# Finer first chunks, a small first parameter load, and two vector steps moved into the retention

## The chip, the cores and the metric

The kernel runs on one core of a Trainium2 chip. The metric is the device time of one execution in microseconds (us). TensorE is PE in the profile, VectorE DVE, ScalarE ACT, GpSimd POOL and SyncE SP.

## The reference

Two blocks of a language model are computed one after the other for 256 tokens of width 1024, in float32. The first puts 16 meta tokens ahead of the input, normalises the rows, and projects them to queries, keys, values and gates; it has a retention with rotary positions (8 heads of 128), a recurrence, and a feed-forward part. The second has three more mixing branches and a mixture of experts. What the change touches stands at the beginning of the first block:

```
h = concatenate([meta, x])                      # 272 rows
u = h * rsqrt(mean(h * h) + eps) * mix_norm_w   # first norm
q, k, v, g_ret, lru_in, ... = split(u @ w_in)
q, k = rotary(q), rotary(k)
o = chunk_retention(q, k, v)                    # per head: scores, decay, scores @ v
c = causal_depthwise_conv(lru_in)               # 4 taps
r = rg_lru(c, ..., lru_lambda)                  # uses softplus(-lru_lambda)
```

## The kernel before

Every matrix product is made of three matmuls: each operand is split into a high and a low half (`whi`, `wlo` for weights), and high x high, high x low and low x high are summed in a PSUM bank. The weights come as pieces of 1 MB, 128 x 2048 floats, in the fixed order of the table `PIECES` ("k" 4 pieces, "q" 4, "v" 4, "lru_in" 4, "g_ret" 4, ...), into three slots of `raw`. SP issues the transfer of a piece once the slot's old piece is split. ACT rounds it to `whi` (line 1136 in `round_piece`), DVE subtracts to get `wlo` (L1667 in `split_piece`), and PE waits for that split. ACT and DVE do this inside their own programs, which are written out by hand: `feed(engine, n)` splits all pieces up to n at that point of the engine's order, and `full(engine, n)` also waits until PE has used n pieces.

**The start.** PE first runs 19 dummy matmuls (L630). Piece 0 and the transposed input `x_t` are loaded in four chunks (L520, L521), each of two of the eight 128-row feature blocks. For a chunk ACT scales the two blocks of x by the first norm's weights (`W("mixw")`) and rounds them, then rounds a quarter of piece 0; DVE makes both low halves (L1714, L1717); `early_keys` on PE multiplies the chunk. All parameters (`par`, 161 columns, "mixw" the first 8) are loaded by one transfer on ACT's queue (L1177), for which ACT and DVE wait. Piece 1 is split in two halves (L1719, L1721). SP queues, in this order, the chunks, pieces 1 and 2, the identity, the two halves of x, the meta tokens, the other constants and the narrow weights `small_w`. ACT squares x row by row for the norm, DVE makes the inverse roots (L1708), and PE spreads them over a row in `scale_row` (L666, L668), behind the products of piece 1. DVE scales the rotary tables by that row.

**The v products.** After the rotations of q DVE calls `rest_of_head` (L1737): it scales the router columns of the narrow weights (L1740), waits for ACT's rounding of them, subtracts (L1742), and computes the recurrence constant softplus(-lambda) as a chain of small instructions on 128 x 8 elements, each waiting for the last (L1745 to L1757). Only then does `feed(dve, PB["lru_in"] + p + 1)` split further pieces. ACT's part, `narrow_high`, lies at the corresponding place of its own order.

**The retention.** A loop over four pairs of heads, p = 0 to 3. PE makes the scores of two heads, the input product of the recurrence for piece `lru_in` + p (li banks), and then scores times v (L712 to L715, bank `o.p`), for which it waits until the score banks are scaled. DVE for each p: `feed` (the split of a piece), the scaling of both heads' scores (L1790 to L1792, three instructions for a head), from p = 1 a reduction (L1796), then, once ACT has copied the li banks, the convolution of two blocks (L1800, L1802). ACT rounds the convolved blocks and after that the next weight piece, which DVE's `feed` of the next p waits for. The constant is read by ACT much later, behind the recurrence's gates (wait for `lam_ready`); the narrow low half `swlo` by GpSimd's first squares of the retention (as a wait) and by PE in the second block.

Of the kernel before, what the change touches and what calls it, by code (L numbers as in the profile page):

```python
# [5 lines left out]
P = 128  # L6
# [3 lines left out]
KT = D // P  # L10
META = 16
TM = META + T
# [14 lines left out]

PIECES = [("k", 4), ("q", 4), ("v", 4), ("lru_in", 4), ("g_ret", 4), ("lru_gates", 2), ("lru_gate", 4),
# [128 lines left out]
PC, NPAR = columns(PARAMS)  # L157
# [45 lines left out]
def program(nc, weights, x, x_t, meta, mem, consts, params, small_w, slot_w, final_w, wa2_w, out):  # L203
# [8 lines left out]
    with ExitStack() as ctx:  # L212
# [72 lines left out]
        def bc1(a, n):  # L285
# [8 lines left out]
        chunk_loaded = [sem(f"chunk_loaded{j}") for j in range(4)]  # L294
# [10 lines left out]
        meta_loaded, ident_loaded, par_loaded, wa2_loaded, small_loaded = (  # L305
            sem(n) for n in ("meta_loaded", "ident_loaded", "par_loaded", "wa2_loaded", "small_loaded"))
# [254 lines left out]
        def _(pe):  # L561
# [89 lines left out]
            def early_keys(n, names, parts, waits):  # L651
                w = [part.rearrange("p (k c) -> p k c", k=KT) for part in (whi[:, n, :], wlo[:, n, :])]
                outs = [begin(x) for x in names]
                size = KT // parts
                for j in range(parts):
                    pe.wait_ge(*waits(j))
                    for c in range(2):
                        for k in range(size * j, size * (j + 1)):
                            last = product(outs[c][:, 0:TM], both(w, ALL, k, slice(c * P, (c + 1) * P)), both(XU, ALL, k), k == 0, k == KT - 1)
                last.then_inc(pieces_used, 1)  # L660
# [16 lines left out]
            early_keys(0, ["k.0", "k.1"], 4, lambda j: (early_split, j + 1) if j < 3 else (piece_split, 1))  # L677
            early_keys(1, ["k.2", "k.3"], 2, lambda j: (early_split, 4) if j == 0 else (piece_split, 2))
# [453 lines left out]
        def _(act):  # L1132
# [44 lines left out]
            act.dma_start(par[:, :], params).then_inc(par_loaded, 16)  # L1177
            act.wait_ge(zeros_ready, 1)
            A(warmed, zeros[:, 0:1], ACT.Sqrt)
            act.wait_ge(par_loaded, 16)  # L1180
            for j in range(4):
                act.wait_ge(chunk_loaded[j], 32 if j < 3 else 16)
                for k in (2 * j, 2 * j + 1):
                    last = A(XU[0][:, k, :], XR[:, k, :], ACT.Copy, scale=W("mixw")[:, k:k + 1])
                last.then_inc(x_high, 1)
                if j == 3:
                    act.wait_ge(piece_loaded[0], 16)
                quarter = slice(512 * j, 512 * (j + 1))
                A(whi[:, 0, quarter], raw[:, 0, quarter], ACT.Copy).then_inc(early_high if j < 3 else piece_high, 1)
# [466 lines left out]
        def _(dve):  # L1656
# [53 lines left out]
            dve.wait_ge(par_loaded, 16)  # L1710
            for j in range(4):
                dve.wait_ge(x_high, j + 1)
                for k in (2 * j, 2 * j + 1):
                    V.scalar_tensor_tensor(XU[1][:, k, :], XR[:, k, :], W("mixw")[:, k:k + 1], XU[0][:, k, :].bitcast(f32), mult, sub)  # L1714
                dve.wait_ge(*((early_high, j + 1) if j < 3 else (piece_high, 1)))
                quarter = slice(512 * j, 512 * (j + 1))
                V.tensor_tensor(wlo[:, 0, quarter], raw[:, 0, quarter], whi[:, 0, quarter].bitcast(f32), sub).then_inc(early_split if j < 3 else piece_split, 1)  # L1717
            dve.wait_ge(early_high, 4)
# [51 lines left out]
            for k in range(KT):  # L1770
                last = V.scalar_tensor_tensor(XR[:, k, :], XR[:, k, :], W("mixw")[:, k:k + 1], SROW, mult, mult)
            last.then_inc(x_scaled, 1)
            for p in range(4):
                full(dve, PB["q"] + p + 1)
                if p == 1:
                    dve.wait_ge(x_high, 5)
                    V.tensor_tensor(XT[1][:, :, :], XR, XT[0][:, :, :].bitcast(f32), sub).then_inc(x_scaled, 1)
# [3 lines left out]
            rest_of_head()  # L1781

            for p in range(4):
# [9 lines left out]

                if p:
# [724 lines left out]
```

## Time and profile before

| | us |
|---|---|
| median of 3 runs (lowest, highest) | 1081.66 (1081.64, 1082.83) |
| the profiled execution | 1081.13 |
| its span | 1079.0 |
| PE busy | 1066.6 |
| DVE busy | 730.3 |
| ACT busy | 620.0 |

The span goes from the first to the last instruction that the profiler saw; the execution's own time has some 2 us around it. Matmuls are pipelined, so that a busy PE is not PE at its peak, but where PE stands idle the time is lost for the whole kernel if all behind it moves by as much.

### The profile page before, as it was taken

The page shows a single profiled execution, that of the slowest core. Times are in us where ns is not written, and L with a number is a line of the kernel's source. Part 1 is how long each engine was busy: PE and PEld are TensorE (multiplying, and loading weights), DVE is VectorE, ACT ScalarE, POOL GpSimd, SP SyncE. Part 2 cuts the span into 40 slices and gives each one's busy share as a digit, 9 for nine tenths or more (in the row PEclk, how much of TensorE's full clock was granted, in tenths as well). Part 3 has the DMA queues.
Part 4 walks back from the last instruction along what each step waited for, and adds up shares of the span by engine and source line. Part 5 has one row for each costly group of instructions (what it writes and reads, how often), then busy time and mean ns, then how long its engine had stood idle before and what let it go on. Part 6 is the DMA issues. An engine that isn't in the chain of part 4 may idle for free.

```text
span 1079.0 us, 17108 instructions
## 1 busy us (share of the span) xinstructions
PE 1066.6 (99%) x7014; PEld 954.9 (88%) x7014; DVE 730.3 (68%) x823; ACT 620.0 (57%) x735; POOL 52.4 (5%) x41
## 2 busy tenths in 40 slices
PE   9999999999999999999999999999999999999998
PEld 7998889999989999998898777889999978878886
DVE  5974665865765554545765648895445678899996
ACT  7753369664465444443673437775444467777774
POOL 0420100000000000000000000000000002000000
PEclk9999999999999999999999999999999999999999
DMA  9552254654745555555346433434446457999993
GB/s 352 201 196 78 79 195 157 232 199 156 247 164 196 197 193 194 194 194 195 117 157 217 158 99 112 151 124 154 160 169 219 167 198 270 355 381 387 366 396 109
DMA packets 32929, 218.04 MB, mean 202 GB/s; under 512 B 4416, under 2 KB 4672, under 8 KB 7520
## 3 DMA queue, kind: packets, MB, share of 16 engines
q1 hardware_dynamic: 30688, 212.96, 55.1%
q0 software_dynamic: 1616, 2.66, 0.7%
q10 hardware_dynamic: 560, 1.47, 0.3%
q8 instruction: 50, 0.82, 0.3%
q14 instruction: 15, 0.12, 0.0%
HBM read 216.55 MB, written 3.67 MB: 204 GB/s over the span
## 4 chain that ended last, share of the span: by engine, by line
PE 91%; DVE 6%; ACT 1%; DMA 1%; issue 1%; SPq 0%; POOLq 0%; DVEq 0%; ACTq 0%
PE bank L578 27%; PE bank L580 27%; PE bank L579 27%; PE bank L639 2%; DVE wlo L1664 1%; DVE wlo L1667 1%; DMA raw<-weights_dram 1%; PE bank L1045 1%; PE bank L967 1%; PE bank L949 1%; DVE last_lo L1664 1%; PE bank L715 0%; PE bank L880 0%; PE bank L1097 0%; PE bank L712 0%
## 5 line engine op out<-in xcount | busy, mean ns | idle before, releaser
L1667 DVE TENSOR_TENSOR wlo<-raw,whi 128x2048 fp32r<-128x2048 f32 x137 | 313.5, 2294 | 161.1 <-ACT whi L1136 160.8
L1136 ACT ACTIVATE whi<-raw 128x2048 fp32r<-128x2048 f32 (+1 forms) x171 | 319.8, 1875 | 136.3 <-PE bank L580 129.2
L578 PE MATMUL bank<-normedT_hi,whi 128*128 128x256 f32 x640 | 177.6, 278 | 0.0
L579 PE MATMUL bank<-normedT_lo,whi 128*128 128x256 f32 x640 | 177.0, 277 | 0.0
L580 PE MATMUL bank<-normedT_hi,wlo 128*128 128x256 f32 x640 | 177.0, 277 | 0.0
L1136 ACT ACTIVATE buf<-bank 128x512 f32<-128x512 f32 (+5 forms) x147 | 70.9, 526 | 145.9 <-PE bank L580 120.2
L578 PEld LDWEIGHTS bank<-normedT_hi,whi 128*128 128x128 f32 x640 | 120.1, 188 | 1.0 <-issue 0.6
L579 PEld LDWEIGHTS bank<-normedT_lo,whi 128*128 128x128 f32 x640 | 120.3, 188 | 0.7 <-issue 0.2
L580 PEld LDWEIGHTS bank<-normedT_hi,wlo 128*128 128x128 f32 x640 | 120.3, 188 | 0.0
L578 PE MATMUL bank<-xT_hi,whi 128*128 128x256 f32 (+1 forms) x320 | 90.9, 284 | 1.7 <-DVE wlo L1667 1.7
L579 PE MATMUL bank<-xT_lo,whi 128*128 128x256 f32 (+1 forms) x320 | 90.2, 282 | 0.0
L580 PE MATMUL bank<-xT_hi,wlo 128*128 128x256 f32 (+1 forms) x320 | 90.2, 282 | 0.0
L1664 DVE TENSOR_TENSOR wlo<-raw,whi 128x2048 fp32r<-128x2048 f32 x27 | 61.7, 2288 | 5.0 <-ACT whi L1136 5.0
L578 PEld LDWEIGHTS bank<-xT_hi,whi 128*128 128x128 f32 x320 | 60.1, 188 | 3.2 <-DVE wlo L1667 1.9
L579 PEld LDWEIGHTS bank<-xT_lo,whi 128*128 128x128 f32 x320 | 60.2, 188 | 0.0
L580 PEld LDWEIGHTS bank<-xT_hi,wlo 128*128 128x128 f32 x320 | 60.2, 188 | 0.0
L578 PE MATMUL bank<-whi,normedT_hi 128*128 128x512 f32 x144 | 57.6, 400 | 0.4 <-DVE wlo L1667 0.3
L580 PE MATMUL bank<-whi,normedT_lo 128*128 128x512 f32 x144 | 56.5, 392 | 0.0
L579 PE MATMUL bank<-wlo,normedT_hi 128*128 128x512 f32 x144 | 56.4, 392 | 0.0
L578 PE MATMUL bank<-whi,gathered_hi 128*128 128x512 f32 x128 | 51.3, 401 | 0.0
L580 PE MATMUL bank<-whi,gathered_lo 128*128 128x512 f32 x128 | 50.0, 391 | 0.0
L579 PE MATMUL bank<-wlo,gathered_hi 128*128 128x512 f32 x128 | 49.9, 390 | 0.0
(415 smaller groups left out, 2412.9 us busy)
## 6 DMA issues: line engine op xcount, KB each, us to landing
raw<-weights_dram SPq DMA_DIRECT2D x174, 1024.0 KB, 5.0
buf<-weights_dram SPq DMA_DIRECT2D x24, 1024.0 KB, 7.3
buf<-x_t_dram SPq DMA_DIRECT2D x4, 272.0 KB, 4.8
raw<-weights_dram SPq DMA_DIRECT2D x4, 256.0 KB, 5.9
buf<-x_dram SPq DMA_DIRECT2D x2, 512.0 KB, 11.2
buf<-mem_dram ACTq DMA_DIRECT2D x1, 1024.0 KB, 10.7
token_rows<-buf SPq DMA_DIRECT2D x1, 1024.0 KB, 8.7
buf<-final_w_dram POOLq DMA_DIRECT2D x1, 512.0 KB, 4.2
```

What stands on the lines that cost most here:

```text
L578: E.matmul(out_, lh, rh, start=start, stop=False)
L579: E.matmul(out_, lh, rl, start=False, stop=False)
L580: return E.matmul(out_, ll, rh, start=False, stop=stop)
L639: last = E.transpose(b[0:i.shape[1], o:o + n], i, ident[0:n, 0:n])
L949: last = E.matmul(b[:, hh * T:(hh + 1) * T], MQT[:, 2 * h + k, r * P:(r + 1) * P], MKT[:, 2 * h + k, :], start=k == 0, stop=k == 1)
L967: last = E.matmul(b[:, c * T:(c + 1) * T], MV[:, s, h * T + c * P:h * T + (c + 1) * P], MPT[:, h, s, :], start=s == 0, stop=s == 1)
L1045: last = E.matmul(o, part[:, r, k * P:(k + 1) * P], PICK[:, r, lo:hi], start=r == 0 and i == 0, stop=r == RT - 1 and i == 1)
L1136: return S.activation(out_, in_, func, **kw)
L1664: V.tensor_tensor(WLO[split_of(u)], RAW[raw_of(u)], WHI[split_of(u)].bitcast(f32), sub).then_inc(piece_split, 1)
L1667: V.tensor_tensor(wlo[:, n % SLOTS, :], raw[:, n % SLOTS, :], whi[:, n % SLOTS, :].bitcast(f32), sub).then_inc(piece_split, 1)
```

## The change

- The table `EARLY` gives the chunks of the start: one, one, two, two and two feature blocks in place of two each. Loads, ACT's and DVE's splits and PE's `early_keys` go over it. The split of piece 1 in halves stays.
- The transfer on ACT's queue brings only the first norm's weights, 8 columns, to a place of their own (`MIXW`). The full parameters are loaded by SP, behind the identity and ahead of x. DVE waits for them in `narrow_scaled`.
- `rest_of_head` is cut in three. The scaling stays behind the rotations of q; the narrow low half (`narrow_low`) goes into the first pair of the retention (p = 0), and the recurrence constant (`recurrence_constant`) into the third (p = 2), both behind the scaling of the scores.

```diff
--- before.py
+++ after.py
@@ -25,6 +25,7 @@
+EARLY = [range(0, 1), range(1, 2), range(2, 4), range(4, 6), range(6, 8)]
...
+        HEAD = buf[5][:, 0:KT * TM]
         XR = cols(5, TM)
+        MIXW = place("mixw", fixed_at[-1] + starts[4] + 1024 + TM, KT)
...
         @block.sync
         def _(sp):
-            for j in range(4):
-                pair_, quarter = slice(2 * j, 2 * j + 2), slice(512 * j, 512 * (j + 1))
-                sp.dma_start(XR[:, pair_, :], x_t[:, pair_, :]).then_inc(chunk_loaded[j], 16)
-                sp.dma_start(raw[:, 0, quarter], weights[0][:, quarter]).then_inc(chunk_loaded[j] if j < 3 else piece_loaded[0], 16)
+            for j, ks in enumerate(EARLY):
+                cols_, part = slice(ks[0] * TM, (ks[-1] + 1) * TM), slice(256 * ks[0], 256 * (ks[-1] + 1))
+                sp.dma_start(HEAD[:, cols_], x_t[:, cols_]).then_inc(chunk_loaded[j], 16)
+                sp.dma_start(raw[:, 0, part], weights[0][:, part]).then_inc(chunk_loaded[j] if j < len(EARLY) - 1 else piece_loaded[0], 16)
             for n in (1, 2):
                 sp.dma_start(raw[:, n, :], weights[n]).then_inc(piece_loaded[n], 16)
             sp.dma_start(con[:, 0:P], consts[:, 0:P]).then_inc(ident_loaded, 16)
+            sp.dma_start(par[:, :], params).then_inc(par_loaded, 16)
             for r in range(RT):
...
-            early_keys(0, ["k.0", "k.1"], 4, lambda j: (early_split, j + 1) if j < 3 else (piece_split, 1))
-            early_keys(1, ["k.2", "k.3"], 2, lambda j: (early_split, 4) if j == 0 else (piece_split, 2))
+            early_keys(0, ["k.0", "k.1"], EARLY, lambda j: (early_split, j + 1) if j < len(EARLY) - 1 else (piece_split, 1))
+            early_keys(1, ["k.2", "k.3"], [range(0, 4), range(4, 8)], lambda j: (early_split, len(EARLY)) if j == 0 else (piece_split, 2))
...
-            act.dma_start(par[:, :], params).then_inc(par_loaded, 16)
+            act.dma_start(MIXW[:, :], params[:, PC["mixw"][0]:PC["mixw"][1]]).then_inc(mixw_loaded, 16)
             act.wait_ge(zeros_ready, 1)
             A(warmed, zeros[:, 0:1], ACT.Sqrt)
-            act.wait_ge(par_loaded, 16)
-            for j in range(4):
-                act.wait_ge(chunk_loaded[j], 32 if j < 3 else 16)
-                for k in (2 * j, 2 * j + 1):
-                    last = A(XU[0][:, k, :], XR[:, k, :], ACT.Copy, scale=W("mixw")[:, k:k + 1])
+            act.wait_ge(mixw_loaded, 16)
+            for j, ks in enumerate(EARLY):
+                act.wait_ge(chunk_loaded[j], 32 if j < len(EARLY) - 1 else 16)
+                for k in ks:
+                    last = A(XU[0][:, k, :], XR[:, k, :], ACT.Copy, scale=MIXW[:, k:k + 1])
                 last.then_inc(x_high, 1)
...
-            def rest_of_head():
+            def narrow_scaled():
+                dve.wait_ge(par_loaded, 16)
                 dve.wait_ge(small_loaded, 16)
                 router = SWR.rearrange("p (k c) -> p k c", k=KT)[:, :, 88:108]
                 V.tensor_tensor(router, router, bc(W("gffn"), 20), mult).then_inc(small_scaled, 1)
+
+            def narrow_low():
                 dve.wait_ge(small_high, 1)
                 V.tensor_tensor(swlo[:, :], SWR, swhi[:, :].bitcast(f32), sub).then_inc(small_split, 1)
+
+            def recurrence_constant():
                 dve.wait_ge(lam_exp, 1)
...
-            rest_of_head()
+            narrow_scaled()
 
             for p in range(4):
                 feed(dve, PB["lru_in"] + p + 1)
...
+                if p == 0:
+                    narrow_low()
+                if p == 2:
+                    recurrence_constant()
                 if p:
                     dve.wait_ge(o_squared, p)
```

DVE's order behind the rotations of q, before (`par` are the parameters, `small` the small statistics, `buf_71` the narrow weights):

```order
L1764 TENSOR_TENSOR buf_70<-buf_62,con 128x512
L1740 TENSOR_TENSOR buf_71<-buf_71,par 128x8x20 [waits small_loaded]
L1742 TENSOR_TENSOR swlo<-buf_71,swhi 128x864 [waits small_high]
L1745 TENSOR_SCALAR small<-small 128x8 [waits lam_exp]
L1746 RECIPROCAL small<-small 128x8 [waits dve_chain]
...
L1756 TENSOR_SCALAR small<-small 128x8 [waits dve_chain]
L1757 TENSOR_SCALAR small<-small 128x8
L1667 TENSOR_TENSOR wlo<-raw,whi 128x2048 [waits piece_high] x4
L1790 TENSOR_SCALAR buf_69<-bank,con 128x128 [waits scored]
```

and now:

```order
L1772 TENSOR_TENSOR buf_70<-buf_62,con 128x512
L1744 TENSOR_TENSOR buf_71<-buf_71,par 128x8x20 [waits small_loaded,par_loaded]
L1670 TENSOR_TENSOR wlo<-raw,whi 128x2048 [waits piece_high] x4
L1798 TENSOR_SCALAR buf_69<-bank,con 128x128 [waits scored]
L1799 SCALAR_TENSOR_TENSOR buf_69<-bank,con 128x128
L1800 SCALAR_TENSOR_TENSOR buf_69<-bank,con 128x128
```

The low half and the whole chain on 128 x 8 elements are gone from between the scaling of the router columns and the splits.

DVE's order in the third pair of heads, from the end of the first score scaling of its second head, before (`buf_69` scaled scores, `buf_66` and `buf_70` input and result of the convolution):

```order
L1790 TENSOR_SCALAR buf_69<-bank,con 128x128 [waits retained,scored]
L1791 SCALAR_TENSOR_TENSOR buf_69<-bank,con 128x128
L1792 SCALAR_TENSOR_TENSOR buf_69<-bank,con 128x128
L1796 TENSOR_REDUCE small<-buf_71 128x2x2 [waits o_squared]
L1800 TENSOR_SCALAR buf_70<-buf_66,par 128x272 [waits evacuated7,evacuated6]
L1802 SCALAR_TENSOR_TENSOR buf_70<-buf_66,par,buf_70 128x272 [waits dve_chain] x3
...
L1667 TENSOR_TENSOR wlo<-raw,whi 128x2048 [waits piece_high]
L1790 TENSOR_SCALAR buf_69<-bank,con 128x128 [waits retained,scored]
```

and now:

```order
L1798 TENSOR_SCALAR buf_69<-bank,con 128x128 [waits retained,scored]
L1799 SCALAR_TENSOR_TENSOR buf_69<-bank,con 128x128
L1800 SCALAR_TENSOR_TENSOR buf_69<-bank,con 128x128
L1753 TENSOR_SCALAR small<-small 128x8 [waits lam_exp]
L1754 RECIPROCAL small<-small 128x8 [waits dve_chain]
...
L1764 TENSOR_SCALAR small<-small 128x8 [waits dve_chain]
L1765 TENSOR_SCALAR small<-small 128x8
L1808 TENSOR_REDUCE small<-buf_71 128x2x2 [waits o_squared]
L1812 TENSOR_SCALAR buf_70<-buf_66,par 128x272 [waits evacuated7,evacuated6]
...
L1670 TENSOR_TENSOR wlo<-raw,whi 128x2048 [waits piece_high]
```

The chain stands between the scaled scores and the reduction, ahead of this pair's convolution and of the split that follows it.

## Rows read from the trace of the kernel before

**Rows 1.** Page, part 1, and busy time by stretch at 61 to 71 us (PE clock third from last)
```profile
span 1079.0 us, 17108 instructions
...
PE 1066.6 (99%) x7014; PEld 954.9 (88%) x7014; DVE 730.3 (68%) x823; ACT 620.0 (57%) x735; POOL 52.4 (5%) x41
...
61.00:71.00 10.00, 8.34 (x67) 8.10 (x66) 7.63 (x28) 8.83 (x12) 1.31 (x1) 1.00 0.23 94
```

**Rows 2.** Waits of PE: us in total, times, longest us
```profile
PE bank L578 <- DVE wlo L1667: 2.7, 4, 1.7
...
PE bank L578 <- DVE wlo L1719: 0.3, 1, 0.3
```

**Rows 3.** Timeline, 0 to 22 us: start, duration, engine, line, operation, [idle before]
```profile
0.96 7.20 PE L630 MATMUL bank<-idle 128*128 128x512 bf16 x19 [0.96 <-POOL idle L2387]
...
13.07 2.01 ACT L1136 ACTIVATE whi<-raw 128x1024 fp32r<-128x1024 f32 x2 [1.04 <-DMA raw<-weights_dram]
...
14.17 1.23 DVE L1719 TENSOR_TENSOR wlo<-raw,whi 128x1024 fp32r<-128x1024 f32 x1 [1.03 <-ACT whi L1136]
...
15.45 0.40 PE L578 MATMUL bank<-xU_hi,whi 128*128 128x272 f32 x1 [0.32 <-DVE wlo L1719]
...
18.81 1.06 ACT L1136 ACTIVATE buf<-buf 128x1024 f32<-128x1024 f32 x1 [0.23 <-DMA buf<-x_dram]
...
21.12 0.47 DVE L1708 RECIPROCAL small<-small 128x1 f32<-128x1 f32 x3
...
21.74 0.37 PE L666 MATMUL bank<-con,small 16*128 16x16 f32 x2
```

**Rows 4.** DMA queues in 3-3.5, 5.5-6 and 8-9 us: packets, MB, share of 16 engines
```profile
q10 hardware_dynamic: 69, 0.03, 23.9%
...
q1 hardware_dynamic: 60, 0.11, 93.3%
...
q1 hardware_dynamic: 200, 0.41, 108.9%
```

**Rows 5.** Timeline of DVE, 60 to 76 us
```profile
60.88 0.31 DVE L1740 TENSOR_TENSOR buf<-buf,par 128x160 f32<-128x160 f32 x1
...
62.25 1.06 DVE L1742 TENSOR_TENSOR swlo<-buf,swhi 128x864 fp32r<-128x864 f32 x1 [1.06 <-ACT swhi L1136]
...
63.87 0.17 DVE L1745 TENSOR_SCALAR small<-small 128x8 f32<-128x8 f32 x1 [0.56 <-ACT small L1136]
...
68.51 0.17 DVE L1757 TENSOR_SCALAR small<-small 128x8 f32<-128x8 f32 x1
...
68.58 6.69 DVE L1667 TENSOR_TENSOR wlo<-raw,whi 128x2048 fp32r<-128x2048 f32 x3
```

**Rows 6.** Timeline of ACT and of PE, 63 to 71 us
```profile
63.74 1.90 ACT L1136 ACTIVATE whi<-raw 128x2048 fp32r<-128x2048 f32 x1
...
68.67 0.60 PE L639 MATMUL bank<-con,buf 128*128 128x128 f32 x4
...
70.92 0.39 PE L578 MATMUL bank<-xT_hi,whi 128*128 128x272 f32 x1 [1.66 <-DVE wlo L1667]
```

**Rows 7.** Timeline of DVE, 94 to 133 us (retention)
```profile
94.86 0.42 DVE L1800 TENSOR_SCALAR buf<-buf,par 128x272 f32<-128x272 f32 x1 [7.88 <-ACT buf L1136]
...
117.45 0.67 DVE L1796 TENSOR_REDUCE small<-buf 128x4 f32<-128x512 f32 x1
...
119.50 0.42 DVE L1800 TENSOR_SCALAR buf<-buf,par 128x272 f32<-128x272 f32 x1 [1.38 <-ACT buf L1136]
...
129.52 0.34 DVE L1792 SCALAR_TENSOR_TENSOR buf<-bank,con 128x128 f32<-128x128 f32 x1
...
131.82 0.42 DVE L1800 TENSOR_SCALAR buf<-buf,par 128x272 f32<-128x272 f32 x1 [1.37 <-ACT buf L1136]
```

**Rows 8.** Timeline of PE, 130 to 141 us
```profile
130.71 0.29 PE L580 MATMUL bank<-xT_hi,wlo 128*128 128x272 f32 x1
...
140.68 0.50 PE L578 MATMUL bank<-whi,xT_hi 128*128 128x512 f32 x1 [0.41 <-DVE wlo L1667]
```

More of the change, by code:

```diff
@@ L293, in program @@
         piece_high = sem("piece_high")
-        chunk_loaded = [sem(f"chunk_loaded{j}") for j in range(4)]
+        chunk_loaded = [sem(f"chunk_loaded{j}") for j in range(len(EARLY))]
         early_high, early_split = sem("early_high"), sem("early_split")
@@ L304, in program @@
         x_loaded = [sem(f"x_loaded{r}") for r in range(RT)]
-        meta_loaded, ident_loaded, par_loaded, wa2_loaded, small_loaded = (
-            sem(n) for n in ("meta_loaded", "ident_loaded", "par_loaded", "wa2_loaded", "small_loaded"))
+        meta_loaded, ident_loaded, par_loaded, wa2_loaded, small_loaded, mixw_loaded = (
+            sem(n) for n in ("meta_loaded", "ident_loaded", "par_loaded", "wa2_loaded", "small_loaded", "mixw_loaded"))
         out_stored = sem("out_stored")
@@ L653, in early_keys @@
                 outs = [begin(x) for x in names]
-                size = KT // parts
-                for j in range(parts):
+                for j, ks in enumerate(parts):
                     pe.wait_ge(*waits(j))
                     for c in range(2):
-                        for k in range(size * j, size * (j + 1)):
+                        for k in ks:
                             last = product(outs[c][:, 0:TM], both(w, ALL, k, slice(c * P, (c + 1) * P)), both(XU, ALL, k), k == 0, k == KT - 1)
@@ L1175, in turned_high @@
                     last.then_inc(high[name], 1)
-            act.dma_start(par[:, :], params).then_inc(par_loaded, 16)
+            act.dma_start(MIXW[:, :], params[:, PC["mixw"][0]:PC["mixw"][1]]).then_inc(mixw_loaded, 16)
             act.wait_ge(zeros_ready, 1)
             A(warmed, zeros[:, 0:1], ACT.Sqrt)
-            act.wait_ge(par_loaded, 16)
-            for j in range(4):
-                act.wait_ge(chunk_loaded[j], 32 if j < 3 else 16)
-                for k in (2 * j, 2 * j + 1):
-                    last = A(XU[0][:, k, :], XR[:, k, :], ACT.Copy, scale=W("mixw")[:, k:k + 1])
+            act.wait_ge(mixw_loaded, 16)
+            for j, ks in enumerate(EARLY):
+                act.wait_ge(chunk_loaded[j], 32 if j < len(EARLY) - 1 else 16)
+                for k in ks:
+                    last = A(XU[0][:, k, :], XR[:, k, :], ACT.Copy, scale=MIXW[:, k:k + 1])
                 last.then_inc(x_high, 1)
-                if j == 3:
+                if j == len(EARLY) - 1:
                     act.wait_ge(piece_loaded[0], 16)
-                quarter = slice(512 * j, 512 * (j + 1))
-                A(whi[:, 0, quarter], raw[:, 0, quarter], ACT.Copy).then_inc(early_high if j < 3 else piece_high, 1)
+                part = slice(256 * ks[0], 256 * (ks[-1] + 1))
+                A(whi[:, 0, part], raw[:, 0, part], ACT.Copy).then_inc(early_high if j < len(EARLY) - 1 else piece_high, 1)
             act.wait_ge(piece_loaded[1], 16)
@@ L1708, in x_inverse @@
                 V.reciprocal(s, s).then_inc(x_scaled, 1)
-            dve.wait_ge(par_loaded, 16)
-            for j in range(4):
+            dve.wait_ge(mixw_loaded, 16)
+            for j, ks in enumerate(EARLY):
                 dve.wait_ge(x_high, j + 1)
[L1713 to L1718, printed above, removed]
+                for k in ks:
+                    V.scalar_tensor_tensor(XU[1][:, k, :], XR[:, k, :], MIXW[:, k:k + 1], XU[0][:, k, :].bitcast(f32), mult, sub)
+                dve.wait_ge(*((early_high, j + 1) if j < len(EARLY) - 1 else (piece_high, 1)))
+                part = slice(256 * ks[0], 256 * (ks[-1] + 1))
+                V.tensor_tensor(wlo[:, 0, part], raw[:, 0, part], whi[:, 0, part].bitcast(f32), sub).then_inc(early_split if j < len(EARLY) - 1 else piece_split, 1)
+            dve.wait_ge(early_high, len(EARLY))
             V.tensor_tensor(wlo[:, 1, 0:PW // 2], raw[:, 1, 0:PW // 2], whi[:, 1, 0:PW // 2].bitcast(f32), sub).then_inc(early_split, 1)
@@ L1770, in _ @@
             for k in range(KT):
-                last = V.scalar_tensor_tensor(XR[:, k, :], XR[:, k, :], W("mixw")[:, k:k + 1], SROW, mult, mult)
+                last = V.scalar_tensor_tensor(XR[:, k, :], XR[:, k, :], MIXW[:, k:k + 1], SROW, mult, mult)
             last.then_inc(x_scaled, 1)
@@ L1775, in _ @@
                 if p == 1:
-                    dve.wait_ge(x_high, 5)
+                    dve.wait_ge(x_high, len(EARLY) + 1)
                     V.tensor_tensor(XT[1][:, :, :], XR, XT[0][:, :, :].bitcast(f32), sub).then_inc(x_scaled, 1)
```

2 lines of the change are left out of this document (1 added, 1 removed).

## The prediction

> **What bounds the kernel now.** I read the page first: the span is 1079.0 us and TensorE (PE) is busy for 1066.6 of them [rows 1]. So this change can give back only time in which PE stands still in the first 140 us, or add such time. The waits of PE are the next view: over the whole span the longest single one is 1.7 us, on a `wlo` split of VectorE (DVE); on the half piece of the start it is 0.3 [rows 2]. Three places matter.
>
> The start: PE runs 19 dummy matmuls from 0.96 for 7.20 us, to 8.16. Later ScalarE (ACT) rounds the first half of piece 1 at 13.07, after 1.04 us idle until its transfer landed; DVE subtracts at 14.17, and PE begins that piece at 15.45. ACT squares the second half of x at 18.81, after 0.23 us idle for its transfer; the third reciprocal of DVE ends at 21.12 + 0.47 = 21.59, and PE takes the scales at 21.74 [rows 3]. So from 13 us on the start goes at the pace of the transfers. The second place is the v products: DVE works on the narrow weights and the recurrence constant from 60.88 to 68.58, only then splits, and PE, whose transposes began at 68.67, takes its next piece at 70.92 after 1.66 us idle [rows 5, 6]. The third is the retention, at 94 to 141 us, where PE hardly waits [rows 7, 8].
>
> **Chunks of one, one, two, two, two.** The first chunk has half the bytes, so PE could have work by about 7 us. But the 19 dummy matmuls stand ahead of it until 8.16 and their number is unchanged; the products of piece 0 then run out early, and PE waits longer for piece 1. What counts is when piece 1 lands. The change puts 4 transfers with rows of about 1 KB in the place of 2 with rows of 2 KB: 512 packets for 256, 16 more for each of the 16 DMA engines. Their price comes from two rows: 69 packets of the parameter load (644 B each) took 23.9% of 16 engines for 0.5 us, 28 ns each; 200 packets of about 2 KB took 108.9% of 16 engines for 1 us, 87 ns each [rows 4]. The line through both has a fixed part of 0 to 5 ns; counting gaps between small issues I take 0.2 us for 16 packets (bounds 0, and 16 x 87 = 1.4 us if a half packet costs as much as a whole). Against that, the parameter load leaves the front: 8 packets each engine x 28 ns = 0.2 us, of which 8 packets of 32 B take back about as much again, since no row shows packets that small (0 to 0.2). Piece 1 comes at +0.2.
>
> SyncE now issues the full parameter load ahead of x, which puts its 0.2 us in front of both x transfers: x comes at +0.4 to +0.5. ACT already waits 0.23 us for x, and the reciprocals end 0.15 us before PE starts on the scales [rows 3], so nearly all of this reaches PE: **+0.45 us** (bounds -0.3, if the small first packets save time at the head of the queue, and +1.7). The extra ACT and DVE instructions of the finer chunks (one more rounding and one more subtraction) are covered by ACT's 1.04 us idle before 13.07; without that cover they would cost some 0.2 us on ACT.
>
> The Trainium skill speaks against small transfers: "DMA: Bandwidth & Descriptors", in Bandwidth, gives a 64 KB transfer 0.95 us and one of 1 MB 6.15 us; an estimate between them gives 1.3 us for 128 KB and 2.0 for 256 KB, so four small in place of two large would cost 1.3 us where I take 0.2, and the sum below would be 1.1 us higher. Its figures are for another issuing engine, and no run here shows them.
>
> **The narrow low half and the constant leave the place after q.** `narrow_scaled` stays at 60.88 and ACT's part behind it too, so ACT still rounds the piece from 63.74 to 65.64 [rows 6]. DVE stood in its own constant until 68.58 [rows 5]; now it can start the split at about 65.7 and ends it 2.29 us later (one split's time, the first part of the 6.69 for three), at 67.95. PE needs it after its four transposes, at 68.67 + 0.6 = 69.27. The whole wait of **-1.66 us** goes, with 1.3 us to spare. Nothing is late next: the following split ends at about 70.3, one full product before its use.
>
> **The narrow low half, in the first retention pair.** It lands behind the six score scalings, in front of the convolution, where DVE idles 7.88 us until 94.86 [rows 7]; 1.06 us of work [rows 5] costs nothing. Without that cover it would delay the convolution by 1.06 us. GpSimd's squares wait for it, but also for a later ACT result.
>
> **The recurrence constant, in the third pair.** From its first instruction at 63.87 to the split behind it at 68.58 it holds DVE for 4.71 us: 24 instructions of some 0.17 us, nearly all waiting for the one before [rows 5]. It goes in front of the reduction that began at 117.45. Between that reduction and the convolution at 119.50 DVE had only 1.38 us idle [rows 7]. So the reduction begins at 117.45 + 4.71 = 122.16, and the convolution 0.67 later, at 122.83: 3.33 us late. Everything behind it hangs in one chain: ACT's rounding of the convolved pair, ACT's rounding of a weight piece, DVE's split of it, and then the six score scalings of the fourth pair, whose last was at 129.52 + 0.34 = 129.86. It moves to 133.19. PE's product with these scores followed its last input product at 130.71 + 0.13 (one matmul every 0.13 us) = 130.84 [rows 8]. A new wait of 133.19 - 130.84 = 2.35 us stands there.
>
> Part is given back: DVE's reduction of 0.67 comes between, so the fourth convolution goes from 131.82 to 133.86, 2.0 late and not 2.35, and the piece that PE waited 0.41 us for at 140.68 [rows 8] comes 2.0 late too. PE arrives 2.35 later than before, less than 0.1 from it. The 0.41 is thus covered, and the net is 2.35 - 0.4 = **+1.97 us**. Its bounds: 0, if PE turns out not to need these scores first, and 3.33, if the delay of DVE passes whole.
>
> **Sum**, on the profiled execution (1081.13 us): +0.45 - 1.66 + 1.97 = +0.76, so 1081.9. The median of the three runs is 0.5 us above the profiled one, and the measure is taken there: 1081.66 + 0.76 = **1082.4 us**. A measurement of this kernel can tell about 0.2%, or 2.2 us, from no change; this isn't that much.
>
> **Rivals.**
> - *The constant is hidden.* If PE does not come to the fourth pair's scores before DVE has made them, the third term is 0 and the sum is +0.45 - 1.66 = -1.2: 1080.5 us. For it: PE showed no wait at all in the retention before 140 us. Against it: the order puts the constant ahead of the reduction, and the slack is 130.84 - 129.86 = 1.0 us behind a delay of 3.33. Chance 0.13.
> - *Slower: the start is bound by the number of packets.* If a 1 KB packet takes what a 2 KB one does, the 16 more cost 16 x 104 = 1.7 us, at a time between 87 ns and the (93.3% of 16 engines for 0.5 us) / 60 = 124 ns of 5.5 to 6 us [rows 4]; with 0.2 for the parameters +1.9, and the sum is +1.9 - 1.66 + 1.97 = +2.2: 1083.9 us. It decides where x lands over 1.5 us later. For it: in 5.5 to 6 us packets of the same size took 124 ns against 87, so bytes alone don't set their time. Against it: the 28 ns of the 644 B packets. The figures of the Trainium skill given above point the same way. Chance 0.11.
> - *The start gains as well.* If the transfers of the start land 0.6 us earlier and the constant is hidden, -1.66 - 0.6 = -2.3: 1079.4 us. It needs x itself to come earlier, though more stands before it. Chance 0.04.
> - *The clock falls in the new wait.* The granted clock was 1.00 in the stretch that held the 1.66 us wait [rows 1], the upper of the two levels; 2.35 us is longer than any wait shown. One product of 48 matmuls at the lower level would cost its own 48 x 0.13 = 6.2 us again: some 1088 us. Chance 0.03.
>
> **How the numbers follow.** The forecast has 0.69, and its own range is 1081.2 to 1083.6, from +0.1 to +1.1 for the start and a few tenths on the new wait. For 8 in 10 the range takes in half of the first rival and half of the second: 1080.5 to 1084.0; outside are about 0.06, 0.06, 0.04 and 0.03. Faster by over 0.2% (under 1079.5) needs the third rival and part of the first: 0.06. Slower by over 0.2% (over 1083.8) comes from half of the second, the clock and the edge of the forecast: 0.10. The rest, 0.84, is within 0.2%.
>
> **What would show it.** In the profile after: dummy matmuls to 8.16 and the first product right behind; PE's wait before piece 1 longer than before, that piece begun at 15.5 to 15.9; the scales at about 22.2; no wait at the third v product; a new wait of PE of about 2.3 us before the fourth pair's score products (an L712 matmul before, waiting for DVE's score scaling), and none left behind it on the next `wlo`. I am wrong if PE does not wait there (first rival), if x lands more than 1.5 us later (second), or if the wait at the v products is still there.

## The result, and the profile after

| | before | after |
|---|---|---|
| median (lowest to highest), 5 runs each | 1082.53 (1081.64 to 1084.70) | 1088.15 (1088.08 to 1088.47) |
| span of the profiled execution | 1079.0 | 1086.4 |
| PE busy | 1066.6 | 1070.8 |
| mean granted clock of PE | 1.00 | 0.994 |

The ratio is 1.0054 [1.0042, 1.0065]: slower by 5.6 us of medians, and by 7.4 us between the two profiled executions. 1082.4 was forecast, with a range to 1084.0. The waits of PE in the kernel after answer to [rows 2] (us in total, times, longest):

```profile
PE bank L715 <- DVE buf L1800: 3.2, 1, 3.2
PE bank L582 <- DVE wlo L1720: 2.8, 1, 2.8
...
PE bank L582 <- DVE wlo L1670: 0.6, 2, 0.3
```

The wait at the v products is gone (four waits on full pieces, the longest 1.7, are now two of 0.3). Two others stand there, of 3.15 us in the retention and 2.85 in the start, and PE's busy time rose by 4.2 us for the same 7014 matmuls. Busy time by stretch says why (stretch, us, busy time and instructions of PE, PEld, DVE, ACT, POOL, then the granted clock, DMA share and GB/s). The kernel after:

```profile
11.00:14.50 3.50, 3.35 (x15) 3.35 (x16) 3.04 (x7) 2.45 (x6) 0.00 (x0) 0.52 1.00 424
61.00:71.00 10.00, 10.00 (x82) 10.00 (x81) 5.44 (x5) 7.14 (x10) 2.42 (x2) 1.00 0.41 130
134.00:143.00 9.00, 9.00 (x26) 6.72 (x27) 3.99 (x9) 2.36 (x4) 1.44 (x2) 0.50 0.25 103
```

and the kernel before, in the first and the last of these stretches:

```profile
11.00:14.50 3.50, 3.50 (x30) 3.50 (x29) 2.47 (x6) 2.46 (x5) 0.00 (x0) 1.00 0.99 410
...
134.00:143.00 9.00, 8.59 (x38) 6.67 (x37) 6.33 (x8) 7.93 (x8) 2.50 (x2) 1.00 0.15 33
```

In both stretches the clock was 1.00, the upper level (2.4 GHz), and is now 0.50 to 0.52, the lower one (1.2 GHz). PE is busy for all of the 9 us from 134, and does 26 matmuls in them where it did 38. At 61 to 71 us PE stands still no more (10.00 against 8.34 of [rows 1]).

**The start**, timeline of PE, ACT and DVE in the kernel after (answers to [rows 3]):

```profile
0.96 5.83 PE L634 MATMUL bank<-idle 128*128 128x512 bf16 x19 [0.96 <-POOL idle L2399]
...
3.93 0.52 ACT L1139 ACTIVATE xU_hi<-buf,mixw 128x272 fp32r<-128x272 f32 x1 [1.22 <-DMA raw<-weights_dram]
...
6.44 0.48 PE L582 MATMUL bank<-xU_hi,whi 128*128 128x272 f32 x1
...
8.62 0.93 ACT L1139 ACTIVATE xU_hi<-buf,mixw 128x272 fp32r<-128x272 f32 x2 [2.56 <-DMA raw<-weights_dram]
...
11.15 0.60 PE L582 MATMUL bank<-xU_hi,whi 128*128 128x272 f32 x1 [2.85 <-DVE wlo L1720]
...
14.04 2.01 ACT L1139 ACTIVATE whi<-raw 128x1024 fp32r<-128x1024 f32 x2 [1.05 <-DMA raw<-weights_dram]
...
20.09 1.06 ACT L1139 ACTIVATE buf<-buf 128x1024 f32<-128x1024 f32 x1 [0.54 <-DMA buf<-x_dram]
...
22.40 0.47 DVE L1711 RECIPROCAL small<-small 128x1 f32<-128x1 f32 x3
...
23.41 0.39 PE L669 MATMUL bank<-con,small 16*128 16x16 f32 x2
```

The first chunk is there early (ACT takes it at 3.93), the third only at 8.62. ACT waits for transfers all along, and piece 1 comes 0.97 us later than before (14.04 for 13.07), the second half of x 1.28 (20.09 for 18.81), the scales 1.67 (23.41 for 21.74).

**The retention**, timeline of DVE, POOL and PE in the third and fourth pair, the kernel after (answers to [rows 7, 8]; the last row is from behind the retention):

```profile
117.22 0.17 DVE L1753 TENSOR_SCALAR small<-small 128x8 f32<-128x8 f32 x1
...
121.92 0.68 DVE L1808 TENSOR_REDUCE small<-buf 128x4 f32<-128x512 f32 x1
...
122.97 2.42 DVE L1814 SCALAR_TENSOR_TENSOR buf<-buf,par,buf 128x272 f32<-128x272 f32 x3
122.98 1.04 POOL L2413 TENSOR_TENSOR buf<-buf 128x512 f32<-128x512 f32 x1 [9.83 <-ACT buf L1139]
...
125.77 1.57 DVE L1814 SCALAR_TENSOR_TENSOR buf<-buf,par,buf 128x272 f32<-128x272 f32 x3
...
130.49 0.29 PE L584 MATMUL bank<-xT_hi,wlo 128*128 128x272 f32 x1
...
133.38 0.34 DVE L1800 SCALAR_TENSOR_TENSOR buf<-bank,con 128x128 f32<-128x128 f32 x1
...
133.93 0.77 PE L715 MATMUL bank<-buf,buf 128*128 128x128 f32 x2 [3.15 <-DVE buf L1800]
...
166.06 2.29 DVE L1833 TENSOR_TENSOR buf<-buf,buf 128x2048 f32<-128x2048 f32 x1 [2.51 <-ACT buf L1139]
```

The constant's chain takes 121.92 - 117.22 = 4.70 us. Three of the convolution's instructions then take 2.42 us, while GpSimd squares beside them; the next three of the same form take 1.57. PE, in the end 0.22 us ahead of before (130.49 for 130.71), waits 3.15 us. The last row is a landmark: this product of DVE stood at 158.69 in the kernel before. It is 7.37 us late, as much as the whole span, so the loss lies ahead of it. PE's first score product is 133.93 - 130.83 = 3.10 late; between it and the landmark another 4.27 are lost, and the old wait of 0.41 [rows 8] is gone besides: some **4.7 us** are left for the clock. This is a rest by subtraction; e5 below tests it.

### The profile page after: what moved, and what is told of

Read it like the earlier page. It is cut to its first block, busy times and chain, and to the rows that moved or that the text cites. A ratio compares the mean times of both kernels' runs of the same rounds, so it can differ in the third digit from the quotient of the medians.

```text
span 1086.4 us, 17114 instructions
## 1 busy us (share of the span) xinstructions
PE 1070.8 (99%) x7014; PEld 959.4 (88%) x7014; DVE 731.3 (67%) x824; ACT 620.2 (57%) x736; POOL 52.2 (5%) x41
## 4 chain that ended last, share of the span: by engine, by line
PE 91%; DVE 6%; ACT 1%; issue 1%; DMA 1%; SPq 0%; POOLq 0%; DVEq 0%; ACTq 0%
PE bank L582 28%; PE bank L583 27%; PE bank L584 27%; PE bank L643 2%; DVE wlo L1667 1%; PE bank L1048 1%; DVE buf L1814 1%; PE bank L970 1%; PE bank L952 1%; DVE last_lo L1667 1%; DMA raw<-weights_dram 1%; PE bank L883 0%; PE bank L718 0%; PE bank L1100 0%; DVE wlo L1670 0%
## 5 line engine op out<-in xcount | busy, mean ns | idle before, releaser
L1139 ACT ACTIVATE whi<-raw 128x2048 fp32r<-128x2048 f32 (+3 forms) x172 | 320.1, 1866 | 137.4 <-PE bank L584 130.6
## 6 DMA issues: line engine op xcount, KB each, us to landing
buf<-mem_dram ACTq DMA_DIRECT2D x1, 1024.0 KB, 10.5
```

What stands on the lines that cost most here:

```text
L1139: return S.activation(out_, in_, func, **kw)
```

## The experiments

"Old start" is the start of the kernel before. The constant (24 instructions) stands behind q as in the kernel before, or in the first or third pair of the retention.

| | start | constant | median (runs) | ratio to before, 95% |
|---|---|---|---|---|
| e1 | new | first pair | 1081.07 (10) | 0.9991 [0.9981, 1.0001] |
| e2 | old | third pair | 1086.99 (4) | 1.0045 [1.0028, 1.0061] |
| e3 | new | behind q | 1084.36 (6) | 1.0021 [1.0009, 1.0034] |
| e4 | old | first pair | 1080.26 (10) | 0.9983 [0.9973, 0.9993] |
| e5 | old | third pair, 14 dummies in the wait | 1083.09 (10) | 1.0008 [0.9997, 1.0020] |
| e6 | chunks only | behind q | 1083.65 (10) | 1.0013 [1.0004, 1.0023] |
| e7 | small parameter load only | behind q | 1082.71 (10) | 1.0002 [0.9991, 1.0013] |
| e8 | old | 11 instructions in the first, 13 in the third | 1080.96 (10) | 0.9985 [0.9976, 0.9995] |
| e9 | old | third pair, GpSimd's squares later | 1085.26 (5) | 1.0033 [1.0019, 1.0047] |
| e10 | old | third pair, 7 dummies in the wait | 1085.22 (10) | 1.0026 [1.0014, 1.0039] |

### e1, e2, e3 and e4: start and place of the constant, apart

My theory was by now that the constant's place costs most, through PE's wait and the clock behind it; the rival was that the start did it, through late transfers and its own stretch at the lower clock. e1 is the changed kernel with

```diff
                 if p == 0:
                     narrow_low()
-                if p == 2:
                     recurrence_constant()
```

> The changed kernel with the recurrence constant in the first pair of the retention (p = 0) instead of the third. Theory 1 (the loss lies in the constant's place: PE waits 3.15 us in the fourth pair and then runs at half the granted clock for some 8 us, which costs about 4 us more): both are gone, the span falls by about 7 us to 1079 to 1080, the median is 0.0 to 1.0 us below that of the kernel before, no stretch behind 100 us has a clock under 0.95. Rival (the loss lies in the start, whose PE wait of 2.85 us also has a half clock behind it): the time stays above 1086.

e2 is the kernel before with only the three calls of the retention from the change:

```diff
-            rest_of_head()
+            narrow_scaled()
...
+                if p == 0:
+                    narrow_low()
+                if p == 2:
+                    recurrence_constant()
```

> The kernel before with only the retention part of the change: narrow low half at p = 0, recurrence constant at p = 2; chunks and parameter load as before. Theory 1: the wait at the v products (1.66 us) is gone, the wait in the fourth pair (3.1 to 3.3 us) and the half clock behind it (8 us long, 4 us lost) are there without the new start: 5 to 5.5 us slower than before, 1087. Rival (the clock falls there only because the start had lowered it before): the clock stays 1.00 and the result is +1.0 to +1.5 us.

e3 is the changed kernel with both steps back behind `narrow_scaled()`:

> The changed kernel with both steps back behind the rotations of q, so only the chunks and the parameter load are new. Theory 1: PE reaches the scales at 23.4 instead of 21.7 us, +1.7 us, all of which stays: 1083.3 to 1084.2, with a stretch at half clock in 11 to 14 us and the 1.66 us wait at the v products back. Rival (the start costs as much as the whole change): 1088. Second rival (the lateness is absorbed by the wait at the v products): +0.0.

It came to 1084.36 us, just above the range of theory 1. Its profile has the scales at 23.26, a wait of 2.65 us in the start with the clock at 0.50 behind it to about 14 us, and the longest v wait at 1.8 us again.

e4 is e2 with `recurrence_constant()` at p = 0 too:

> The kernel before with narrow low half and constant both in the first pair (p = 0), where DVE idles nearly 8 us. Theory 1: 1.66 to 1.9 us faster than before, 1079.8 to 1080.8, no wait of PE over 0.5 us before 160 us apart from the start. Rival (removing the wait at the v products only moves it on): same as before.

e4 is 6.7 us faster than e2 with the old start (1086.99 - 1080.26), and e1 7.1 faster than the changed kernel with the new one (1088.15 - 1081.07); e1 is even 1.5 us below the kernel before (1082.54), where 0.0 to 1.0 was expected. Nothing but the constant's place differs. e2, with the old start, has the wait and the clock of the changed kernel. First its timeline of PE:

```profile
132.64 0.77 PE L713 MATMUL bank<-buf,buf 128*128 128x128 f32 x2 [3.16 <-DVE buf L1798]
```

and its busy time by stretch:

```profile
134.00:143.00 9.00, 9.00 (x26) 6.82 (x26) 3.19 (x7) 3.64 (x5) 2.35 (x2) 0.50 0.13 55
```

In e4 the same two views, the timeline and then the busy time by stretch, are these; DVE has its 2.19 us of idle time left ahead of the first convolution there, even with the whole chain in that pair.

```profile
139.44 0.51 PE L580 MATMUL bank<-whi,xT_hi 128*128 128x512 f32 x1 [0.41 <-DVE wlo L1668]
```

```profile
134.00:143.00 9.00, 8.59 (x37) 6.70 (x37) 6.36 (x8) 8.51 (x8) 2.51 (x2) 1.00 0.28 86
```

The 0.41 us of [rows 8] is back, the clock is 1.00, and the landmark stands at 157.47. So the wait of 3.15 us together with the lower clock is the loss of the change, and both come from the third pair. e4 has the lowest median of all versions; by the ratios it can't be told from e8 (0.9983 and 0.9985).

The new start costs 1081.07 - 1080.26 = 0.8 us between e4 and e1, 1.2 between e2 and the changed kernel, and 1.8 between the kernel before (1082.54 in that comparison) and e3. Only the last is clear of the spread; the intervals of e1 and e4 overlap, as those of e2 and the changed kernel do. In e1 the dummy matmuls took 7.14 us, PE waited only 0.76 and 0.99 us in the start and kept its clock (busy time by stretch):

```profile
11.00:14.50 3.50, 3.40 (x27) 3.19 (x26) 2.63 (x6) 1.85 (x5) 0.00 (x0) 1.00 1.00 422
```

Still its scales came at 23.44, as in the changed kernel (23.41). The lower clock of the start thus hid behind the transfers; what the start costs is their lateness.

### e6 and e7: which half of the new start

e6 is the kernel before with the table of five chunks alone, all parameters still first; e7 keeps the four chunks and takes the small parameter load with the full one behind the identity:

```diff
-EARLY = [range(0, 2), range(2, 4), range(4, 6), range(6, 8)]
+EARLY = [range(0, 1), range(1, 2), range(2, 4), range(4, 6), range(6, 8)]
```

> The kernel before with the chunks of one, one, two, two, two alone; the full parameters still come first on ACT's queue and both steps stay behind the rotations of q. If the smaller rows make the transfers slow: piece 1 is rounded at 14.0 (before 13.07), x comes about 1 us late, the scales at 22.6 to 23.2, +1 to +1.5 us. Rival (the parameters in front of x cost the time): piece 1 within 0.2 us of before, +0.0 to +0.3 us.

```diff
-            act.dma_start(par[:, :], params).then_inc(par_loaded, 16)
+            act.dma_start(MIXW[:, :], params[:, PC["mixw"][0]:PC["mixw"][1]]).then_inc(mixw_loaded, 16)
...
+            sp.dma_start(par[:, :], params).then_inc(par_loaded, 16)
```

> The kernel before with the small first parameter load alone, chunks of two each, the full parameters ahead of x on SP's queue, both steps behind the rotations of q. If the smaller rows of the chunks were what cost time: piece 1 at 12.8 to 13.1, x +0.3 us, the scales at 22.0 to 22.1: +0.3 us. Rival (the parameters' transfer costs over 1 us where it stands now): the scales at 22.7 or later.

In e6 piece 1 is rounded at 14.16, x is squared at 19.91 and the scales come at 23.17; in e7 these are 13.71, 19.81 and 22.74; before, 13.07, 18.81 and 21.74. So the chunks bring 1.1 us at piece 1, and either half about 1 us at x. One execution is no exact measure of these: the profiles of the six other kernels with the old start (e2, e4, e5, e8, e9, e10) have the scales anywhere from 21.58 to 22.41, and piece 1 rounded from 12.90 to 13.46. The four profiles with the finer chunks (after, e1, e3, e6) lie outside on both, at 23.17 to 23.44 and 13.92 to 14.17. For e7 I had expected piece 1 at 12.8 to 13.1 and the scales at 22.0 to 22.1. It is beyond both, and its scales are where its rival had them, at 22.7 or later; the median shows nothing of it. Over all, the chunks cost 0.13%, and the small load nothing that can be measured.

e7's profile shows something else. It has the old wait at the v products and none in the retention, and yet its clock fell there, in a stretch in which PE had no idle time at all (timeline of PE, e7):

```profile
110.42 0.48 PE L718 MATMUL bank<-buf,buf 16*128 16x128 f32 x2
110.83 1.22 PE L697 MATMUL bank<-buf,buf 128*128 128x256 f32 x2
111.84 0.64 PE L698 MATMUL bank<-buf,buf 128*128 128x128 f32 x2
```

The 128x256 products take 1.22 us for two from 110.83 on, where two took 0.70 in the kernel before. Busy time by stretch:

```profile
112.00:113.00 1.00, 1.00 (x5) 0.91 (x4) 0.12 (x1) 0.84 (x2) 1.00 (x2) 0.50 0.00 0
```

PE had been on the retention's small products since 107.16 us. What this says of the prediction stands further down.

### e5 and e10: idle time or late scores

e5 is e2 with dummy matmuls in the wait, so that PE has something to do, and the scores are as late as in e2; e10 has 7 of them.

```diff
                 b = begin(f"o.{p}")
+                if p == 3:
+                    spin(b, 14)
                 moved(pe, f"s.{2 * p}"
```

> The kernel of e2 (old start, constant in the third pair) with 14 dummy matmuls on PE in front of the wait of the fourth pair, into that pair's own bank. Theory 1 (the wait and the clock behind it are two prices, 3.2 us and 4.1 us, the second because PE stands idle): the dummies of 0.21 us fill 3.0 of the 3.16 us, the clock stays 1.00 behind 131 us, PE starts the pair at the same time after its last input product as in e2, and the time is about 4 us under e2: 1082.5 to 1083.5. Rival (the half clock comes from something else, as DVE or the transfers): the clock falls as in e2, about 1087.

> The kernel of e5 with 7 dummy matmuls in place of 14, so that PE stands idle for some 1.6 us of the 3.16 us wait. The start of the fourth pair doesn't move. If the length of the idle time lets the clock fall: it stays 1.00 (1.66 us before did no harm) and the time is that of e5, 1083. Rival (any unfilled rest of that wait brings the half clock): 1087 as in e2.

Timeline of PE, e5, with the 14 dummies and the first of the scores:

```profile
129.76 3.20 PE L632 MATMUL bank<-idle 128*128 128x512 bf16 x14
132.96 0.46 PE L715 MATMUL bank<-buf,buf 128*128 128x128 f32 x2
```

and busy time by stretch, e5:

```profile
134.00:143.00 9.00, 9.00 (x43) 6.94 (x43) 6.10 (x10) 6.17 (x6) 2.37 (x2) 1.00 0.19 76
```

PE begins with the scores 0.32 us later than in e2, does 43 matmuls in 9 us where e2 did 26, and reaches the landmark at 160.40 instead of 165.52. The median falls by 1086.99 - 1083.09 = 3.9 us. That is what the dummies give back, by runs, and it is rather too little for the clock: only three of e5's ten executions had a mean clock of 1.000, the others 0.996 to 0.999. The profiled executions say 5.4: from the scores to the landmark e5 takes 27.44 us, e2 32.88. The wait alone leaves the kernel at the time of before. The timeline of PE in e10:

```profile
129.46 1.69 PE L632 MATMUL bank<-idle 128*128 128x512 bf16 x7
132.66 0.46 PE L715 MATMUL bank<-buf,buf 128*128 128x128 f32 x2 [1.51 <-DVE buf L1800]
```

and its busy time by stretch:

```profile
137.00:140.00 3.00, 3.00 (x9) 2.32 (x8) 0.31 (x2) 3.00 (x4) 2.35 (x2) 0.51 0.02 5
```

Here PE resumes at the full clock, and the clock falls only some 4 us later, for about 3.5 us. I had expected 1.51 us of idle time to leave it alone, since 1.66 us at the v products does (clock 1.00, [rows 1]). It didn't, and the median lies between the two that I had named (1083 and 1087); the ten runs spread from 1082.40 to 1087.35 us, and the interval overlaps that of e2. So the length of the idle time doesn't decide alone.

### e8 and e9: how much fits, and the collision with GpSimd

e8 leaves the chain's last 13 instructions in the third pair and does the first 11 in the first:

```diff
-                for d in (13, 11, 9, 7, 5, 3, 1):
+                for d in (13, 11, 9):
...
+            def constant_end():
...
+                for d in (7, 5, 3, 1):
```

> Old start; the first 11 of the constant's 24 instructions in the first pair, the last 13 in the third. By the chain's 0.205 us an instruction the third pair's reduction begins 2.65 us late and its convolution 1.3 us late. If DVE and GpSimd get in each other's way there as in the changed kernel (three instructions took 2.42 us in place of 1.58 while GpSimd's squares ran), 2.1 us late, and PE waits 1.1 to 1.3 us; if not, 0.3 us. The clock stays 1.00 in both. Time 1080.5 to 1081.5; rival (every wait there brings the half clock): over 1084.

e9 is e2 with GpSimd's squares of the third pair behind its low half of the convolution:

```diff
+                if p != 2:
+                    squares_of(p)
                 pool.wait_ge(high["conv"], p + 1)
...
+                if p == 2:
+                    squares_of(p)
```

> The kernel of e2 (old start, constant in the third pair) with GpSimd's squares of the third pair moved behind its low half of the convolution, out of the time in which DVE convolves. If GpSimd's squares held DVE up: the three convolution instructions that took 2.42 us take 1.58 again, the wait of the fourth pair falls from 3.16 to 2.3 us. Whether the clock falls behind 2.3 us no run has shown: if it does, the time is 0.8 us under e2, 1086.2; if not, 1082 to 1083. Rival (DVE was held up by something else): 2.42 and 3.16 us as in e2.

In e8 the wait shrinks to 0.67 us, where I had 1.1 to 1.3 with a collision and 0.3 without, and the clock of the profiled execution is 1.00 (timeline of PE, e8):

```profile
130.02 0.46 PE L713 MATMUL bank<-buf,buf 128*128 128x128 f32 x2 [0.67 <-issue]
```

The collision moves with the squares: 0.67 us (2.24 for 1.57) land on the second block's instructions in e8, in e9 none on the convolution, but 0.46 on the split (2.75 for 2.29). Timeline of DVE and POOL in e8:

```profile
119.25 1.57 DVE L1819 SCALAR_TENSOR_TENSOR buf<-buf,par,buf 128x272 f32<-128x272 f32 x3
...
121.19 2.24 DVE L1819 SCALAR_TENSOR_TENSOR buf<-buf,par,buf 128x272 f32<-128x272 f32 x3
121.56 1.04 POOL L2418 TENSOR_TENSOR buf<-buf 128x512 f32<-128x512 f32 x1 [9.83 <-ACT buf L1137]
```

and in e9:

```profile
122.04 1.57 DVE L1812 SCALAR_TENSOR_TENSOR buf<-buf,par,buf 128x272 f32<-128x272 f32 x3
...
127.65 1.04 POOL L2412 TENSOR_TENSOR buf<-buf 128x512 f32<-128x512 f32 x1
128.09 2.75 DVE L1668 TENSOR_TENSOR wlo<-raw,whi 128x2048 fp32r<-128x2048 f32 x1 [2.53 <-ACT whi L1137]
```

Three times over, a GpSimd operation of 1.04 us takes 0.84, 0.67 or 0.46 us from what DVE does at that moment. The Trainium skill says this in "SBUF — State Buffer", Who interferes with whom: a DVE instruction with two inputs in SBUF and a GpSimd instruction that reads SBUF exclude each other, and whoever comes first holds the port. These traces agree: all DVE instructions here that grew have two such inputs. In e9 the wait is still 2.75 us and not the 2.3 I had expected, since the squares now hold up the split; PE resumes at the full clock at 132.60, which falls at about 134.5 and is 0.50 until about 141. The time, too, lies between the two that I had named. It is 1.7 us of medians below e2 (1086.99 - 1085.26), but with 4 and 5 runs the intervals overlap.

## Why the prediction was wrong

- **What bounds the kernel: right.** All of the 7.4 us lie in the first 166 us, in PE's idle time and clock.
- **v products, -1.66: right.** The wait is gone, and PE's balance from the scales (+1.67) to the end of the fourth input product (-0.22) says -1.89, a bit more than the term. DVE began the split at 67.38, and PE its transposes at 70.36 (68.67 before): both are 1.7 us later than said, by what the start lost, and the order between them held.
- **Low half in the first pair, 0: right.** It stands at 86.68 in an idle stretch; DVE idled 6.91 us where it had 7.88.
- **Start, +0.45: mis-sized, it is +1.67** in the profile and 0.8 to 1.8 us in medians. The step that failed is "Piece 1 comes at +0.2": it came 0.97 us late after the change and 1.09 in e6. I took the price of a small packet from a parameter load and gave the four transfers' extra packets 0.2 us, with all that follows at its old pace. The price itself was not far off: from 3 to 4 us the queue of the weights moved 252 packets of about 1 KB after the change in 87.4% of 16 engines, 55 ns each, against 151 of about 2 KB before in 89.5%, 95 ns (72 ns for 1 KB in e6). But the packets of about 2 KB behind them slowed down. DMA queue in 7 to 8 us, first before, then after:

```profile
q1 hardware_dynamic: 195, 0.37, 101.5%
...
q1 hardware_dynamic: 124, 0.23, 101.4%
```

That is 83 ns a packet before and 131 after. From 2 to 11 us this queue moved 2.52 to 2.60 MB in the four profiles with the finer chunks and 2.80 to 2.95 in the eight with the old ones, and 0.39 MB less after the change than before, about 1 us of its work. Why the larger packets behind the small ones take longer, no run shows. The Trainium skill's "DMA: Bandwidth & Descriptors" (Bandwidth), by whose figures I had estimated 1.3 us (the recorded terms, four times 1.3 against two times 2.0, make 1.2), was much nearer. "PE waits longer for piece 1" was wrong in place: the wait came ahead of the third chunk. The dummy matmuls ended at 6.79 and not at 8.16, since they came 0.43 us apart only up to 4.25 us and 0.2 us apart from there (before, up to 7 us). That looks like the lower and the upper clock, but the profile's granted clock reads 1.00 for both, so it isn't shown. In e1 the same 19 took 7.14 us, and in e4 with the old start 5.70, so this isn't the change's doing. My own rival of the packets (+1.9) is the case that x's 1.28 us and the 1.67 of the scales are nearest to in size; its reason, a 1 KB packet as dear as one of 2 KB, is not what the trace has.
- **Constant in the third pair, +1.97: place, chain and direction right, size wrong twice.** The chain took 4.70 us where 4.71 was said, and the wait stood where it was forecast. It was 3.15 and not 2.35: the step "the reduction begins at 117.45 + 4.71 = 122.16, and the convolution 0.67 later, at 122.83: 3.33 us late" went on as if DVE's instructions kept their durations, while the convolution now ran beside GpSimd's squares, which wait for ACT and did not move with DVE (+0.84). Before, those squares began at 123.20, when the convolution was nearly done, at 123.49. That gives 3.15 - 0.41 = 2.74, and the clock another 4.7 (next point).
- **The clock: the step that did most of the damage.** The sum has no term for it; it stood as a rival at a chance of 0.03, on the ground that "the granted clock was 1.00 in the stretch that held the 1.66 us wait". But the clock fell to 0.50, and that took some 4.7 us (e5 gives back 3.9 by medians, 5.4 by profiles). I had priced it at 6.2 us for one product, so its "some 1088" hit 1088.15 by luck in part: two errors, of the start and the wait, stood in for the difference. The terms of the profiles add up to what was measured (+0.76 forecast, +1.22 start, +0.8 wait, +4.7 clock is 7.5, and 7.4 was measured), but as the 4.7 is itself a rest, this proves nothing; e5 and e4 are the check. A harmless wait of 1.66 us said too little of one of 2.35 or more. In the start of e6 the clock fell after a wait of 2.36 us, ahead of the long product of piece 0, where no small products follow (timeline of PE, then busy time by stretch, e6):

```profile
10.83 0.39 PE L580 MATMUL bank<-xU_hi,whi 128*128 128x272 f32 x1 [2.36 <-DVE wlo L1718]
...
11.00:14.50 3.50, 3.50 (x18) 3.50 (x19) 2.94 (x6) 2.20 (x5) 0.00 (x0) 0.54 1.01 427
```

What follows the wait may count besides: the v wait stands ahead of a product of 48 matmuls that follow one another at 0.13 us each, the new one ahead of small products, 20 matmuls in 3.75 us, and there 1.51 us was enough in e10 (all one execution each).

**A second lesson lies in the runs of the kernel before.** The profiled execution on which the sum was built had a mean clock of 1.00. Of 64 executions of the kernel before in these comparisons, 18 had 1.000 (median 1081.3 us), 29 had 0.998 (median 1083.2), and the other 17 had 0.997 or 0.999. e7's profile is of the second kind (0.998, 1083.49 us, clock at 0.50 from about 110.8 to 114.2), while the e7 executions with 1.000 took 1081.0 to 1081.9 us. Whether the kernel before loses its 1.9 us at the same spot, no profile here shows; e3 and e6, whose profiles have 0.997 and 0.998 with the constant behind q as before, lost it in the start. The executions at the lower mean clock fit a gap in the numbers: the profiled executions differ by 7.4 us, the medians by 5.6, and the kernel before has this loss in part of its runs and in its profile not.

**What stays open.** What decides whether the clock falls after a wait. Observed in the profiled executions, one each, were:

- no fall behind waits of 1.66 us at the v products, of 0.76 to 1.82 us in the start (e1, e2, e4, e5, e7, e8, e9), of 0.67 in the retention (e8), and with none at all there (e5);
- a fall in the start behind 2.36 us (e6), 2.65 (e3) and 2.85 (after), for some 3 us;
- a fall in the retention behind 3.15 (after) and 3.16 us (e2), present already when PE resumed; behind 2.75 (e9), some 2 us after it; behind 1.51 (e10), some 4 us after it; and in e7 with no wait.

The lower clock held for about 3.5 us in e10, 7 in e9, 10.5 after the change and 12.5 in e2, counted from where PE resumed or the clock fell. From the scores to the landmark these four take 28.84, 30.30, 32.13 and 32.88 us against e5's 27.44: 1.4, 2.9, 4.7 and 5.4 us. So the price goes with the length of the stretch, and that differs by 2 us between two waits of the same length. Whether e4 too loses time in some executions by such a fall (its mean clocks go from 0.997 to 1.000) wasn't looked at.

## What to carry to other kernels

Before small work is moved on a helper engine, rank the places by the idle time that this engine has there: the same 4.7 us chain cost nothing ahead of a convolution with 7.9 us idle, and 7 us of time where it had 1.4. A new wait of TensorE is priced at its length and, beside it, at a possible stretch of half clock behind it. Every wait of TensorE over 2.3 us in these profiles brought one, and a shorter, harmless wait elsewhere is no proof against it. Whether small products behind a wait are worse than a long dense one is only suggested here, by 1.51 us against 1.66 and 1.82. Work that moves on VectorE moves against GpSimd's: see which of its operations will run beside it now.

## What the runs showed of the hardware

- PE's granted clock fell to 0.50 after 1.51 us of idle time ahead of small products (e10), after 2.36 us ahead of a long product (e6), and once with no idle time (e7), but not after 1.66 us ahead of a long product. It fell up to 4 us after PE had resumed.
- 14 dummy matmuls in a wait of 3.2 us kept it at 1.00 in the profiled execution and gave back 3.9 us of medians; with 7 of them it was 1.8 us, which the spread doesn't resolve.
- The same 19 dummy matmuls at the start took 5.83 us after the change and 7.20 before, 7.14 and 5.70 in e1 and e4: a fixed number of them doesn't end at a fixed time.
- A GpSimd square of 128x512 beside DVE's instructions with two SBUF inputs took 0.46 to 0.84 us from them.
- With two early transfers of 2 KB rows cut into four of 1 KB rows, piece 1 was rounded at 13.92 to 14.17 us in four profiles, against 12.90 to 13.71 in eight; the loss showed in the 2 KB packets behind, 131 ns each in 7 to 8 us where they had taken 83.
